# Latent attention heads in one pipeline over three token pieces, with values weighed by unsplit fp32 matmuls

## The chip, the cores and the metric

The kernel runs on one core of one Trainium2 chip. Its engines are TensorE (PE in the profile; PEld is its weight load), VectorE (DVE), ScalarE (ACT), GpSimd (POOL) and the DMA queues. The metric is the time of one execution on the device in microseconds. The kernel before takes 3545.39 us (median of 3 runs, 3545.22 to 3548.24).

## The reference, cut to what matters

A first block (windowed attention, convolution, a recurrence, a wide feed-forward) is followed by two layers that each contain latent attention. The change is in the heads of those two layers; the rest is the same code.

```python
T = 1040 tokens (16 meta tokens and 1024), 8 heads, 2 layers, all float32
q  = (c_q  @ w_q_b ).reshape(T, 8, 96)            # c_q : 768 channels, normalised
kv = (c_kv @ w_kv_b).reshape(T, 8, 64 + 64)       # c_kv: 256 channels, normalised
k_nope, v = kv[..., :64], kv[..., 64:]
k  = concatenate([k_nope, k_rope of all heads])   # 96 wide
q, k = rmsnorm(q), rmsnorm(k)                     # over the 96
q, k = rope on the last 32 of each
s = q @ k.T / sqrt(96), causal                    # 1040 x 1040 for each head
o = softmax(s) @ v
y_mla = (o * silu(z_mla)) @ mla_w_up
```

## The kernel before, in words

Activations lie with channels on partitions and tokens along the free dimension (1044 columns, the last four empty). An fp32 product is made of three matmuls with rounded operands (fp32r): high by high, high by low, low by high. The stored low part of an operand is the operand less its rounded value. Weights come as a stream of units of 128 x 1024. SyncE loads unit n+2 when GpSimd has split unit n; GpSimd casts a unit to its high part and subtracts for the low part (L322, L324), after TensorE has reported the unit two places before it as used. One unit holds a head's query and key/value weights.

Each engine has an order of instructions written out by hand, tied by semaphores; nothing is reordered by a planner. PSUM has `acc`, two slots of three banks, and `aux`, two banks. In the head stage (8 heads in each of 2 layers) a head is done so:

- `head_key_value`, `head_query` (L578, L583; matmuls at L353): 24 weight tiles, each over three pieces of 348 tokens, into one slot each. ScalarE squares and copies the whole width (`head_key_squares`, `head_query_squares`), TensorE sums squares with a matrix of ones in plain fp32 (`head_sum`, L587, L591), ScalarE takes log and exponential (`head_log`, L1066, and `head_exp`, L1072), VectorE applies the rope table, the scale and the split of query and key (`head_table`, `head_query`, `head_key`, L1601 to L1621, over 1044 columns at once).
- `rough_scores` (L605, matmuls L613, L617): high parts alone, rows of 128 queries, to get an upper row maximum; VectorE reduces (`maxima`, L1662). `head_values` transposes the values (L601), which ScalarE and VectorE store as V1 and V2. The nine columns of maxima are turned into one row (L686) that is put into an unused row of the query, so that later scores come with their maximum subtracted.
- `scores_t` (L620, matmuls L629, L633): scores transposed, keys on partitions, three matmuls per tile. There are 15 blocks of at most 384 columns (`BLOCKS`), in five batches of three; batch b has slot 1 - b % 2. ScalarE computes each block's exponential twice, once as fp32 and once rounded (L1145, L1146); VectorE subtracts for the low part (`low_parts`, L1648).
- `weigh_values` (L637, matmuls L648): three matmuls per tile into `aux`; the other 64 columns of V1 are ones, so the sum of a row comes with it. `head_inverse` (ScalarE) and `head_out` (VectorE, L1659, L1660) divide.

The next head's key, query and sums stand between rough scores and scores of this head; the last six blocks' values stand inside the next head's rough scores. VectorE waits once in each layer for the spill of `work` to memory (`g_spilled`) after its first `head_table`.

## Time and profile before

| | us |
|---|---|
| median of 3 runs | 3545.39 |
| lowest, highest | 3545.22, 3548.24 |
| span of the profiled execution | 3557.2 |
| PE busy | 3139.6 |
| DVE busy | 1569.9 |
| ACT busy | 711.5 |
| POOL busy | 833.7 |

For the profiled execution only its span is given, from its first to its last instruction, and that span is the profiled execution's own time here. It is 11.8 us above the median of the runs. Busy is the time in which an engine has a record; a TensorE record contains the delay until its result is written, so consecutive records overlap and the distance of their starts is the cost of one. The two head stages lie at about 1901 to 2320 us and 2987 to 3408 us. The mean granted clock of TensorE over the span is 0.929, where 1.00 is 2.4 GHz and 0.50 is 1.2 GHz.

### The profile page before, as it was taken

To read this page: it belongs to the slowest core of one execution; us is meant where nothing else is said; L and a number is where in the kernel's file an instruction comes from. 1 tells how busy PE (TensorE), PEld (TensorE's weight loads), DVE (VectorE), ACT (ScalarE), POOL (GpSimd) and SP (SyncE) were. 2 spreads that over 40 slices of the span, in tenths; PEclk is the share of its full clock that TensorE was granted. 3 is DMA by queue.
4 is the path that set the end of the run, shared out by engine and by line. 5 is a ranking of instruction groups with operands and counts; after the bars stand their busy time and mean duration, and the time that the engine had idled before them with its cause. 6 is when DMAs were issued, how large, how long until landed. Compare 5 with 4: busy or idle time off the path is not lost.

```text
span 3557.2 us, 40295 instructions
## 1 busy us (share of the span) xinstructions
PE 3139.6 (88%) x16640; PEld 2803.0 (79%) x16640; DVE 1569.9 (44%) x1540; ACT 711.5 (20%) x1191; POOL 833.7 (23%) x646
## 2 busy tenths in 40 slices
PE   6975676999999995999997888898999997888899
PEld 4754565777777774999997787798999997877789
DVE  4677456333333336500115665663520114655671
ACT  2132310000000002000112454400000111544410
POOL 2321012233333331333322000022333332000012
PEclk9987789999999997999998888899999998988899
DMA  2100011111111111112112000042112112000131
GB/s 98 47 30 27 0 71 38 47 46 43 47 47 41 47 47 66 54 42 96 48 42 77 8 13 13 31 152 94 42 48 90 48 42 84 13 13 7 37 145 71
DMA packets 46201, 182.47 MB, mean 51 GB/s; under 512 B 5744, under 2 KB 5872, under 8 KB 45552
## 3 DMA queue, kind: packets, MB, share of 16 engines
q1 hardware_dynamic: 31248, 113.19, 10.0%
q10 hardware_dynamic: 14816, 67.28, 4.9%
q8 instruction: 108, 1.77, 0.2%
q14 instruction: 29, 0.24, 0.0%
HBM read 150.06 MB, written 30.39 MB: 51 GB/s over the span
## 4 chain that ended last, share of the span: by engine, by line
PE 70%; DVE 20%; ACT 4%; issue 3%; DMA 1%; POOL 1%; DVEq 0%; ACTq 0%; SPq 0%; POOLq 0%
PE acc L353 61%; PE aux L648 2%; DVE act_lo L1214 2%; DVE ff_split L1214 2%; DVE small L1665 2%; DVE ff_split L1213 1%; DVE residual L1279 1%; PE acc L629 1%; PE acc L613 1%; DVE act_hi L1213 1%; DVE work L1230 1%; DMA spill_g<-work 1%; DVE work L1223 1%; ACT pool_split L1146 1%; PE aux L686 1%
## 5 line engine op out<-in xcount | busy, mean ns | idle before, releaser
L353 PE MATMUL acc<-act_hi,w_hi 128*128 128x348 f32 (+1 forms) x3488 | 868.4, 351 | 106.0 <-DVE act_lo L1214 39.2
L353 PE MATMUL acc<-act_lo,w_hi 128*128 128x348 f32 (+1 forms) x3488 | 855.7, 347 | 0.0
L353 PE MATMUL acc<-act_hi,w_lo 128*128 128x348 f32 (+1 forms) x3488 | 853.0, 346 | 0.0
L353 PEld LDWEIGHTS acc<-act_hi,w_hi 128*128 128x128 f32 x3488 | 619.3, 193 | 168.1 <-issue 70.5
L321 POOL TENSOR_TENSOR small<-shape_consts 128x1 f32<-128x1 f32 x212 | 47.1, 222 | 2666.4 <-PE acc L353 2666.4
L353 PEld LDWEIGHTS acc<-act_lo,w_hi 128*128 128x128 f32 x3488 | 624.4, 193 | 44.0
L353 PEld LDWEIGHTS acc<-act_hi,w_lo 128*128 128x128 f32 x3488 | 620.8, 192 | 42.1
L324 POOL TENSOR_TENSOR w_lo<-w_raw,w_hi 128x1024 fp32r<-128x1024 f32 x212 | 568.1, 2680 | 17.0
L353 PE MATMUL acc<-ff_split,w_hi 128*128 128x512 f32 (+1 forms) x1408 | 356.6, 379 | 22.0 <-DVE ff_split L1214 22.0
L1431 DVE TENSOR_TENSOR residual<-acc,residual 128x1024 f32<-128x1024 f32 (+1 forms) x88 | 108.1, 1229 | 468.2 <-PE acc L353 468.2
L353 PEld LDWEIGHTS acc<-ff_split,w_hi 128*128 128x128 f32 x1408 | 257.6, 190 | 71.1 <-DVE ff_split L1214 26.5
L322 POOL CAST w_hi<-w_raw 128x1024 fp32r<-128x1024 f32 x212 | 220.8, 1041 | 0.0
L648 PE MATMUL aux<-pool_split 128*128 128x276 f32 (+5 forms) x864 | 154.1, 332 | 60.7 <-DVE pool_split L1648 60.5
L353 PE MATMUL acc<-ff_split,w_lo 128*128 128x512 f32 (+1 forms) x704 | 202.4, 376 | 0.0
L648 PEld LDWEIGHTS aux<-pool_split 128*128 128x128 f32 x864 | 136.6, 217 | 68.8 <-DVE pool_split L1648 41.6
L629 PE MATMUL acc<-ff_split 128*128 128x276 f32 (+5 forms) x864 | 165.8, 336 | 1.9 <-issue 1.9
L957 ACT ACTIVATE work<-acc 128x1024 f32<-128x1024 f32 x32 | 32.8, 1028 | 642.5 <-PE acc L353 641.9
L629 PEld LDWEIGHTS acc<-ff_split 128*128 128x128 f32 x864 | 150.7, 221 | 5.5 <-issue 2.6
L1223 DVE TENSOR_TENSOR work<-work 128x1044 f32<-128x1044 f32 (+1 forms) x47 | 73.4, 1562 | 174.1 <-ACT work L763 172.9
L353 PEld LDWEIGHTS acc<-ff_split,w_lo 128*128 128x128 f32 x704 | 129.6, 189 | 23.9
L1665 DVE TENSOR_REDUCE small<-acc 128x1 f32<-128x128 f32 (+2 forms) x144 | 116.9, 812 | 67.7 <-PE acc L617 62.6
L613 PE MATMUL acc<-ff_split 128*128 128x512 f32 (+4 forms) x240 | 91.3, 460 | 57.9 <-DVE small L1665 30.6
(215 smaller groups left out, 2887.3 us busy)
## 6 DMA issues: line engine op xcount, KB each, us to landing
w_raw<-in_wstream SPq DMA_DIRECT2D x215, 512.0 KB, 3.5
spill_x<-residual ACTq DMA_DIRECT2D x2, 4176.0 KB, 12.7
spill_m<-residual ACTq DMA_DIRECT2D x2, 4176.0 KB, 13.2
spill_g<-work ACTq DMA_DIRECT2D x2, 4176.0 KB, 14.3
residual<-spill_m ACTq DMA_DIRECT2D x16, 522.0 KB, 5.9
work<-spill_g ACTq DMA_DIRECT2D x16, 522.0 KB, 7.9
residual<-spill_x ACTq DMA_DIRECT2D x16, 522.0 KB, 4.3
residual<-in_xT ACTq DMA_DIRECT2D x8, 512.0 KB, 9.9
```

Of the source, the lines that this page charges most:

```text
L321: nc.gpsimd.tensor_tensor(S_[:, 62:63], C_[:, 128:129], C_[:, 128:129], ALU.add)
L322: nc.gpsimd.tensor_copy(Wh[:, s, :], Wraw[:, s, :]).then_inc(sems["w_hi_done"], 1)
L324: nc.gpsimd.tensor_tensor(Wl[:, s, :], Wraw[:, s, :], Wh[:, s, :].bitcast(F32), ALU.subtract).then_inc(sems["w_lo_done"], 1)
L353: ins = nc.tensor.matmul(acc[0:m, s, p, 0:w], wt[:, ws, w0 + j * m:w0 + j * m + m], x[:, k, p * w:p * w + w], start=(first and t == 0), st ...
L613: ins = nc.tensor.matmul(acc[:, s, p, 0:n], qh[:, min(P * i, LASTQ):min(P * i, LASTQ) + P], kh[:, 512 * p:512 * p + n], start=True, stop=n ...
L629: ins = nc.tensor.matmul(out, k2[kt][:, c0:c0 + P], q2[qt][:, lo:lo + w], start=m == 0, stop=(m == 2 and not diag))
L648: ins = nc.tensor.matmul(aux[:, pc % 2, lo - QP * pc:lo - QP * pc + w], v[:, t, :], prob(n, part)[:, at:at + w], start=(t == 0 and m == 0) ...
L1213: do(vec.tensor_copy(hi, src))
L1214: do(vec.tensor_tensor(lo, src, hi.bitcast(F32), ALU.subtract), name)
L1223: do(vec.tensor_tensor(total, total, slots[1 + j % 2][:, cols], ALU.add), "sum_ready" if j == n - 1 else "sq_free" if j <= n - 3 else "dve ...
L1431: do(vec.tensor_tensor(x, acc_view(s, pieces), x, ALU.add), f"free{s}")
L1665: do(vec.tensor_reduce(S_[:, 16 + i:17 + i], acc[:, s, :, :].rearrange("p a b -> p (a b)")[:, 0:min(P * (i + 1), TP)], AX, ALU.max, negate ...
```

## The change

The head stage is written again for all engines. Tokens go in three pieces of 384, 384 and 276 columns (`QP`, `NQP`, which existed for the blocks). `acc` is used by bank: `acc_q`, `acc_k`, `acc_n` (sums and turned values), two of scores `acc_s`, and `acc_r` (rough scores, one bank, a rough row of over 512 keys in two or three parts with a maximum each). A pass over `h` runs through the 15 blocks of head h and, beside block n, does a fixed part of the preparation of head g = h + 1; a pass h = -1 comes first. The values of block n - 2 are weighed in step n. Every hand-over has its own semaphore, where `free`/`ready` pairs and `to_dve` were shared.

Probabilities are written once, as plain fp32 (`prob(k)`, a ring of 6), and the values once for each of two heads (`values(h)`); one matmul takes both as they are. The second exponential, `low_parts` and V2 are gone. Temporary arrays of a piece's width have two buffers. GpSimd's loop over weight units is cut into loops and single splits around the heads, without other waits. The wait for `g_spilled` stands before VectorE's first table operation.

Core of the diff (TensorE):

```diff
-                        for m, (v, part) in enumerate(((V1, 0), (V1, 1), (V2, 0))):
-                            ins = nc.tensor.matmul(aux[:, pc % 2, lo - QP * pc:lo - QP * pc + w], v[:, t, :],
-                                                   prob(n, part)[:, at:at + w],
-                                                   start=(t == 0 and m == 0), stop=(end and m == 2))
+                        ins = nc.tensor.matmul(aux[:, b % 2, lo - QP * pc:lo - QP * pc + w], values(h)[:, t, :],
+                                               prob(k)[:, at:at + w], start=t == 0, stop=end)
...
+                for h in range(-1, MH):
+                    g = h + 1
+                    more = g < MH
+                    for n in range(NB):
+                        if h >= 0:
+                            scores(h, n)
+                            if n == 0:
+                                turn_maxima(h, 1)
+                            if n in (1, 2, 3):
+                                rough_scores(h, 5 + n, 0)
+                            if n == 4:
+                                rough_scores(h, 8, 2)
+                            if n == 5:
+                                turn_maxima(h, 2)
+                        if more:
+                            if n in (8, 9, 10):
+                                rough_scores(g, n - 8, 0)
+                            if n == 11:
+                                turn_maxima(g, 0)
+                            if n in (12, 13, 14):
+                                rough_scores(g, n - 9, 0)
+                            if n in (0, 4, 8):
+                                key_value_part(g, n // 4)
+                            elif n < 12:
+                                query_part(g, n // 4, n % 4 - 1)
+                            if n in (3, 7, 11):
+                                key_sum(g, n // 4)
+                            if n in (4, 8, 12):
+                                query_sum(g, n // 4 - 1)
+                            if n in (6, 10, 13):
+                                turn_values(g, (n - 6) // 3)
+                            if n in (13, 14):
+                                rough_scores(g, n - 9, 1)
+                        if h >= 0 and n in (1, 2, 3):
+                            rough_scores(h, 5 + n, 1)
+                        if h >= 0 and n >= 2:
+                            weigh_values(h, n - 2)
+                        if h >= 1 and n < 2:
+                            weigh_values(h - 1, NB - 2 + n)
```

Waits of a sum, of the turned maxima and of the turned values (one bank each, `n_free` and `r_free` being the last reader):

```diff
+                def query_sum(g, pc):
...
+                    pe.wait_ge(*n_free[0])
+                    pe.wait_ge(sems["q_squared"], k)
+                    nc.tensor.matmul(acc_n[:, 0:w], ones96, qsq[k % 2][:, 0:w], start=True,
+                                     stop=True).then_inc(sems["q_sum"], 1)
+                    n_free[0] = (sems["qn_free"], k)
...
+                def turn_maxima(h, pc):
...
+                    pe.wait_ge(*r_free[0])
+                    if pc:
+                        pe.wait_ge(sems["max_ready"], 2 * (l * MH + h) + pc)
...
+                def scores(h, n):
...
+                    if k > 2:
+                        pe.wait_ge(sems["p_in"], k - 2)
+                    if tiles[0][0] == 0:
+                        pe.wait_ge(sems["max_row"], wave(l, h, pc))
+                        pe.wait_ge(sems["k_lo"], wave(l, h, pc))
+                        pe.wait_ge(sems["q_lo"], wave(l, h, pc))
```

ScalarE's order and VectorE's order in the same steps:

```diff
+                            exponents(h, n)
+                            if n == 0:
+                                maximum_row(h, 1)
+                            if n == 2 and h >= 1:
+                                inverse_sums(h - 1, 2)
+                            if n == 4:
+                                inverse_sums(h, 0)
+                            if n == 5:
+                                maximum_row(h, 2)
+                            if n == 9:
+                                inverse_sums(h, 1)
...
+                            if n == 11:
+                                maximum_row(g, 0)
+                            if n in (4, 8, 12):
+                                key_scale(g, n // 4 - 1)
+                            if n in (0, 4, 8):
+                                key_value_evict(g, n // 4)
+                            if n in (5, 9, 13):
+                                query_scale(g, n // 4 - 1)
+                            if n in (7, 11, 14):
+                                values_in(g, (n - 7) // 3)
+                            if n in (3, 7, 11):
+                                query_squares(g, n // 4)
...
+                            if n == 3 and h >= 1:
+                                head_out(h - 1, 2)
+                            if n in (1, 2, 3):
+                                maximum(h, 5 + n, 0)
+                                maximum(h, 5 + n, 1)
+                            if n == 4:
+                                maximum(h, 8, 2)
+                                maxima_of(2)
+                            if n == 5:
+                                head_out(h, 0)
+                            if n == 10:
+                                head_out(h, 1)
...
+                            if n in (4, 8, 12):
+                                query_table(g, n // 4 - 1)
+                            if n in (5, 9, 13):
+                                key_norm(g, n // 4 - 1)
+                            if n in (6, 10, 14):
+                                query_norm(g, (n - 6) // 4)
+                            if n in (8, 9, 10):
+                                maximum(g, n - 8, 0)
+                            if n in (12, 13, 14):
+                                maximum(g, n - 9, 0)
+                            if n in (13, 14):
+                                maximum(g, n - 9, 1)
+                            if n == 14:
+                                maxima_of(1)
```

`query_table` is three VectorE operations on a piece (rope table from PSUM, a copy of 32 rows, an addition on 32 rows), `key_norm` four, `query_norm` three, `head_out` two.

## Rows read from the trace of the kernel before

**Rows 1.** The page: busy us (share of the span) and instructions of each engine.
```profile
PE 3139.6 (88%) x16640; PEld 2803.0 (79%) x16640; DVE 1569.9 (44%) x1540; ACT 711.5 (20%) x1191; POOL 833.7 (23%) x646
```

**Rows 2.** Stretches of one head; PEclk is the granted clock.
```profile
core 0: us, PE busy (x) PEld busy (x) DVE busy (x) ACT busy (x) POOL busy (x), PEclk, DMA share, GB/s
1971.05:2022.24 51.19, 45.05 (x254) 40.78 (x253) 30.75 (x42) 24.16 (x50) 3.53 (x3) 0.87 0.04 11
2008.59:2012.01 3.42, 1.95 (x12) 1.75 (x10) 3.32 (x4) 2.79 (x7) 0.00 (x0) 1.00 0.00 0
2018.83:2022.24 3.41, 1.39 (x11) 1.39 (x12) 3.24 (x6) 1.33 (x5) 0.00 (x0) 1.00 0.00 0
2022.24:2025.66 3.42, 3.42 (x18) 3.42 (x17) 0.89 (x2) 1.54 (x4) 0.00 (x0) 0.50 0.00 0
2032.48:2035.90 3.42, 1.90 (x9) 1.16 (x7) 3.28 (x5) 0.00 (x0) 0.00 (x0) 1.00 0.00 0
2035.90:2039.31 3.41, 3.14 (x10) 2.95 (x11) 2.68 (x3) 0.00 (x0) 0.00 (x0) 0.50 0.02 5
```

**Rows 3.** Waits of that head: us in total, times, longest.
```profile
POOL small L321 <- PE acc L353: 47.7, 1, 47.7
PE aux L648 <- DVE pool_split L1648: 3.9, 2, 2.3
PEld acc L613 <- DVE small L1665: 3.2, 5, 1.4
PE acc L613 <- DVE small L1665: 2.2, 4, 1.2
```

**Rows 4.** Timeline of TensorE at full clock: start, us, record.
```profile
2051.37 0.64 PE L353 MATMUL acc<-act_lo,w_hi 128*128 128x348 f32 x3
2051.85 0.63 PE L353 MATMUL acc<-act_hi,w_lo 128*128 128x348 f32 x3
2052.32 1.92 PE L591 MATMUL acc<-residual,shape_consts 128*128 128x348 f32 x6
2054.16 1.91 PE L686 MATMUL aux<-shape_consts,small 128*1 128x128 f32 x18
2056.00 2.02 PE L591 MATMUL acc<-residual,shape_consts 128*128 128x348 f32 x6
...
2277.79 0.45 PE L629 MATMUL acc<-ff_split 128*128 128x20 f32 x3
2278.10 0.26 PE L633 MATMUL acc<-pool_split 128*128 128x20 f32 x1
...
2280.41 1.54 PE L648 MATMUL aux<-pool_split 128*128 128x276 f32 x12
...
2298.32 2.32 PE L629 MATMUL acc<-ff_split 128*128 128x384 f32 x12
```

**Rows 5.** Groups of that head by form: busy us, mean ns, idle before.
```profile
L1648 DVE TENSOR_TENSOR pool_split<-work,pool_split 128x384 fp32r<-128x384 f32 x7 | 3.9, 558 | 0.4 <-ACT pool_split L1146 0.2
L1145 ACT ACTIVATE work<-acc 128x384 f32<-128x384 f32 x7 | 3.5, 497 | 1.0 <-DVE pool_split L1648 0.8 <-PE acc L629 0.3
L1648 DVE TENSOR_TENSOR pool_split<-work,pool_split 128x276 fp32r<-128x276 f32 x7 | 3.1, 446 | 0.4
L1213 DVE CAST ff_split<-residual 128x1044 fp32r<-128x1044 f32 x2 | 1.4, 704 | 0.1
L1610 DVE SCALAR_TENSOR_TENSOR residual<-residual,params 128x1044 f32<-128x1044 f32 x1 | 1.3, 1305 | 0.0
L1665 DVE TENSOR_REDUCE small<-acc 128x1 f32<-128x512 f32 x1 | 0.7, 692 | 0.0
L1092 ACT ACTIVATE work<-work 64x384 f32<-64x384 f32 x1 | 0.5, 523 | 0.0
```

**Rows 6.** Timeline around GpSimd's split of a unit, and the copy alone.
```profile
1892.02 3.33 DVE L1214 TENSOR_TENSOR act_lo<-work,act_hi 128x1044 fp32r<-128x1044 f32 x1
...
1909.24 0.69 DVE L1603 COPY residual<-residual 32x1044 f32<-32x1044 f32 x1
...
2052.69 1.04 POOL L322 CAST w_hi<-w_raw 128x1024 fp32r<-128x1024 f32 x1
2053.81 2.35 POOL L324 TENSOR_TENSOR w_lo<-w_raw,w_hi 128x1024 fp32r<-128x1024 f32 x1
2054.94 1.77 DVE L1603 COPY residual<-residual 32x1044 f32<-32x1044 f32 x1
```

**Rows 7.** Timeline at the start and end of the head stage of layer 0.
```profile
1916.00 0.43 DVE L1679 CAST pool_split<-shape_consts 128x512 fp32r<-128x512 f32 x1 [4.80 <-DMA spill_g<-work]
...
2319.73 0.57 PE L353 MATMUL acc<-ff_split,w_hi 128*128 128x348 f32 x2
```

More of the change, by code:

```diff
@@ L620, in scores_t, with key_value_part @@
-                def scores_t(n, s, b, q2, k2):
+                n_free, r_free = [None], [None]
+                def key_value_part(g, pc):
+                    k = wave(l, g, pc)
+                    c0, w = QP * pc, piece_width(pc)
+                    if pc == 0:
+                        w_head[0] = ws()
+                        next_unit()
+                    if k > 1:
+                        pe.wait_ge(sems["k_free"], k - 1)
+                    for j in range(2):
+                        if g == 0 and pc == 0:
+                            pe.wait_ge(sems["a_ready"], a_count + j + 1)
+                        for t, (wt, x) in enumerate(((Wh, Ah), (Wh, Al), (Wl, Ah))):
+                            ins = nc.tensor.matmul(acc_k[:, 0:w], wt[:, w_head[0], (6 + j) * P:(7 + j) * P],
+                                                   x[:, 6 + j, c0:c0 + w], start=(j == 0 and t == 0),
+                                                   stop=(j == 1 and t == 2))
+                    ins.then_inc(sems["kv_raw"], 1)
@@ new lines, in query_part @@
+                def query_part(g, pc, part):
+                    k = wave(l, g, pc)
+                    c0, w = QP * pc, piece_width(pc)
+                    if part == 0 and k > 1:
+                        pe.wait_ge(sems["q_free"], k - 1)
+                    for j in (2 * part, 2 * part + 1):
+                        if g == 0 and pc == 0:
+                            pe.wait_ge(sems["a_ready"], a_count + j + 3)
+                        for t, (wt, x) in enumerate(((Wh, Ah), (Wh, Al), (Wl, Ah))):
+                            ins = nc.tensor.matmul(acc_q[:, 0:w], wt[:, w_head[0], j * P:j * P + P],
+                                                   x[:, j, c0:c0 + w], start=(j == 0 and t == 0),
+                                                   stop=(j == 5 and t == 2))
+                    if part == 2:
+                        ins.then_inc(sems["q_raw"] if pc < NQP - 1 else sems["unit_done"], 1)
@@ new lines, in key_sum @@
+                def key_sum(g, pc):
+                    k = wave(l, g, pc)
+                    c0, w = QP * pc, piece_width(pc)
+                    if n_free[0] is not None:
+                        pe.wait_ge(*n_free[0])
+                    pe.wait_ge(sems["k_squared"], k)
+                    nc.tensor.matmul(acc_n[:, 0:w], ones96, X[:, 6, c0:c0 + w], start=True,
+                                     stop=True).then_inc(sems["k_sum"], 1)
+                    n_free[0] = (sems["kn_free"], k)
@@ new lines, in turn_maxima @@
+                def turn_maxima(h, pc):
+                    pe.wait_ge(*r_free[0])
+                    if pc:
+                        pe.wait_ge(sems["max_ready"], 2 * (l * MH + h) + pc)
+                    for i in range(3 * pc, 3 * pc + 3):
+                        n = min(P, TP - P * i)
+                        o = P * (i - 3 * pc)
+                        ins = nc.tensor.matmul(acc_r[32:33, o:o + n], S_[:, 16 + i:17 + i], ident[:, P - n:P],
+                                               start=True, stop=True)
+                    ins.then_inc(sems["max_turned"], 1)
+                    r_free[0] = (sems["max_row"], wave(l, h, pc))
@@ L622, in scores_t @@
                     at = 0
-                    for j, lo, w in BLOCKS[n][1]:
-                        out = acc[:, s, b, at:at + w]
+                    for j, lo, w in tiles:
+                        out = acc_s[k % 2][:, at:at + w]
                         at += w
@@ L1651, in head_out @@
                 def head_out(h, pc):
[L1653 to L1655 removed]
+                    k = wave(l, h, pc)
+                    dve.wait_ge(sems["inv_ready"], k)
                     w = piece_width(pc)
@@ L1723, in _ @@
-                low_parts(4)
-                head_out(MH - 1, 1)
+                for h in range(-1, MH):
+                    g = h + 1
+                    more = g < MH
+                    for n in range(NB):
+                        if h >= 0:
+                            if n == 3 and h >= 1:
[10 more added lines that the diff above has]
+                                head_out(h, 1)
+                            if n in (6, 8) and not more:
+                                j = n // 2 - 3
+                                split(X[:, j, :], Fy[0][:, j, wide], Fy[1][:, j, wide], "f_ready")
+                        if more:
+                            if n in (4, 8, 12):
[12 more added lines that the diff above has]
+                                maxima_of(1)
```

579 lines of the change are left out of this document (259 added, 320 removed).

## The prediction

> **What bounds the kernel now.** I read the page's busy times first, then the TensorE clock by stretches of one head, then the waits of that head, then its timeline. TensorE is busy for 3139.6 us of a span of 3557.2 [rows 1], so time can come only from its work, its clock or its gaps. The change touches one stage, the attention heads: 16 heads (8 in each of two layers), about 51.2 us each. In one such head (the first of [rows 2]) TensorE has 45.05 us of records and 6.1 us without any, and a mean granted clock of 0.87. The short stretches say where: in three of those shown TensorE has records for 1.95, 1.39 and 1.90 of 3.4 us. After the first the clock stays at 1.00 (2.4 GHz); the other two are followed by 0.50 (1.2 GHz), each time for two stretches of 3.4 us. 13.6 us per head at 1.2 GHz, nearly all filled, cost half of that, 6.7 us. So a head is 38.3 us of work at full clock, 6.7 us of low clock and 6.2 us of gaps. The gaps are hand-overs [rows 3]: the first weighing of values in a piece waits for VectorE's low parts (3.9 us), rough scores for VectorE's maxima (2.2 us on TensorE, 3.2 on its weight loads).
>
> **The change part by part.** All durations are starts to starts at full clock.
>
> 1. *Values product.* Removed: 36 of 54 matmuls per head, 15 ScalarE exponentials (the second copy), 15 VectorE subtractions (about 7.3 us busy; 0.56 and 0.45 us each [rows 5]) and the value low parts. Added: nothing but the matmul's own kind. The rounded form costs 0.16 us per 348 columns (three start 0.48 apart), 0.175 at 384 (twelve in 2.32 us), 0.13 at 276, and does not fall below 0.103 for 20 columns (three, then the next start 0.31 us later) [rows 4]. The unrounded form appears as two records per matmul; six records of 348 columns take 1.92 us to the end of the last, 1.84 to the next start, so 0.29 a record and 0.58 a matmul, 0.64 at 384, 0.46 at 276; at 128 columns 18 records take 1.84, so 0.21 a matmul [rows 4]. A head has 18 tiles: 5 of 384, 7 of 276, 2 of 256, 4 of 148 or less. Before: 3 x (5 x 0.175 + 7 x 0.13 + 2 x 0.122 + 4 x 0.105) = 7.4 us. After: 5 x 0.64 + 7 x 0.46 + 2 x 0.427 + 0.9 = 8.1 us. So the product itself gets 0.7 us per head slower; bounds 0 (if the small tiles hide their weight loads) and +2.5 (below).
> The Trainium skill ("FP8 and Floating Point Precision", section "TensorE Precision Notes") says that true fp32 takes four passes through the array. Four in place of three would make it 7.4 x 4/3 = 9.9 us, +2.5. The rows above say +0.7, because the rounded form pays a floor on small tiles that the unrounded one does not; I take the rows, and +2.5 is a rival below.
>
> 2. *Pieces.* Query, key and sum matmuls become 384, 384 and 276 columns wide where they were 348 three times: 24 groups of 0.175 + 0.175 + 0.13 = 0.48 us, as before. Nothing. Rough scores, transposes and causal adds are the same instructions. TensorE's work by the new order, summed over its 15 steps: scores 8.3, values 8.1, rough 3.5, turned maxima 1.9, query and key 11.5, sums 3.5, turned values 0.8: 37.8 us.
>
> 3. *One pipeline.* Each step issues scores of block n, a part of the next head and the values of block n-2. So the gaps must be found again. A hand-over TensorE to X to TensorE costs X plus some 0.3 us (the tail of the last record and two starts). I walked one head with ScalarE at 0.49 us (384) and 0.40 (276), VectorE at 0.56 and 0.45 (0.62 for the scaled product and 0.36 for a cast at 384, brought down from 1.31 and 0.70 at 1044 by the slope of the rows; 0.69 for a maximum over 512) [rows 5], and VectorE's and ScalarE's queues in the order of the diff. What ends late:
> - n=4: the query sum waits until ScalarE has read the key sum, and ScalarE has the exponential (0.49) and the inverse of the sums (0.49 and 0.52) ahead of that 0.49: 1.0 us.
> - n=8: the same without the inverse: 0.15.
> - n=11: the maxima are turned only when VectorE has reduced rough tile 2, behind the head output and the query of piece 1: 1.0; then the key sum behind ScalarE's copies: 0.3.
> - n=12, 13: query sum behind ScalarE (0.7), turned values behind ScalarE (0.8), rough tile 4's second half (0.2).
> - n=14: the second half of rough tile 5 behind VectorE's query of piece 2 and a maximum: 1.1.
> Together 5.3 us of gaps, and VectorE, 27.8 us busy by the same rows, is the late one from n=10 to n=14, where it has 10.9 us of work beside 10.0 us of TensorE's (PE steps n=10 to 14).
>
> 4. *GpSimd.* It splits one weight unit per head: cast 1.04 us, subtraction 2.35 us, started by the end of the head's query product [rows 6]. While it runs, VectorE operations that read only SBUF stand: a copy of 32 x 1044 takes 1.77 us beside it and 0.69 alone, and a subtraction of 1044 takes 3.33 where 1.25 is usual [rows 6]. The new order ends the query product at n=11, right ahead of VectorE's rope addition for piece 2 and all that follows, which is the late chain: +2.1 us (bounds 0 and 2.4). The loop over units cut in several costs nothing: GpSimd waits 47.7 of 51.2 us [rows 3].
>
> A head is then 37.8 + 5.3 + 2.1 = 45.2 us at full clock.
>
> 5. *First and last pass.* VectorE starts at 1916.0 when the spill has landed, as before [rows 7], now ahead of its first query. The first pass has no scores to fill it; VectorE's 20 us come in a chain with TensorE's and ScalarE's at low clock: I get the first scores at 1947.8. Seven passes of 45.2 less 0.9 (the first has no old head to finish), and a last pass of 24.2 us (8.3 + 8.1 + 1.8 + 1.2 us of work, and three steps with two maxima each, 1.0 us of waiting apiece, 1 us at the end): 1947.8 + 315.5 + 24.2 = 2287.5. Before, the next stage's matmuls start at 2319.7 [rows 7]. That is 32 us for a layer, 64 for both (I take layer 1 to repeat it).
>
> 6. *Clock.* From n=11 to n=14 of the new order TensorE has 7.8 us of work in 14.1. Its thinnest stretches resemble those of 1.95 and 1.90 us above, of which one kept the clock and the other lost it. One fall of 6.8 us there costs about 2.2 us, since part of it lies in gaps. Bounds: 0 and 2 falls in filled work, 6.7 us. I take a fall in half of the heads: 1.1 x 14 = 15 us.
>
> Sum: 64 - 15 = 49 us off the profiled 3557.2. That execution is 11.8 us above the median of the three runs, 0.3%; taken off the median 3545.4 it gives 3496.
>
> **The rivals.**
> - *Clean pipeline.* GpSimd's hold misses VectorE's chain and the clock stays: 43.1 us a head. For it: VectorE's total is far below TensorE's. Against: the split starts exactly there. 64 + 2 x 15 = 94 off: 3452.
> - *Slower: the clock is lost in filled work.* Many short waits keep TensorE thin enough, from n=9 until the next head's query parts, to be at 1.2 GHz for as long as now (13.6 us a head, 6.7 us lost), all of it beside dense work, on top of 45.2: 51.9. The first pass already costs 21.6 us that the old order did not have before its first scores (against 10 won in the last). 7 x 51.9 = 363.3 against 315.5 + 0.9: 47 more than above in a layer, 15 slower than before (32 won): 3545 + 30 = 3575. It decides from 49.8 us a head, where the 32 us of a layer are used up. For it: two of three thin stretches lose the clock now. Against: the dense steps n=0 to n=8 have no gap over 1 us.
> - *Four passes.* The unrounded product costs 9.9 us in a head: 1.8 x 16 = 29 more: 3525. Against: the 0.29 us record of 348 columns; for: full-width weights are loaded for each record, which the 128-column row has not.
> - *It does not do what it says*: the gaps and low clock only move, since TensorE's work is no less than now (37.8 us against 38.3), and a head ends near 49.8. That is 3545, no change. Against: the walk finds 7.4 us of gaps where 12.9 are now lost.
>
> **How the numbers follow.** Forecast 0.55 (3496, own range 3470 to 3525), clean 0.18 (3452), four passes 0.12 (3525), lost clock 0.12 (3575), no change 0.03. Below 3435 would need a head under 42 us, 4 of gaps. Range 3435 to 3560, which leaves out most of the lost clock and a little of the clean case. A change under 0.2% (7 us) can't be told from none. Faster: 0.84 (a little of the third case lost to its spread); same 0.04; slower 0.12.
>
> **What would show it.** The values matmuls: 36 records a head, 0.23 us apart at 276 columns and 0.32 at 384, not more. The distance of the same instruction in neighbouring heads: 45 to 46.5 us; under 44 clean, over 49.8 slower. A VectorE addition over 32 rows of about 2.5 us once a head beside GpSimd's subtraction. TensorE's waits in n=11 to n=14 on VectorE, in n=4 on ScalarE. Clock 1.00 through n=0 to n=8. The first scores 21 us later than the first rough scores now, the stage's end 2285 to 2300 in layer 0. Wrong would be: waits at each score for exponentials (I have none), or values products waiting for GpSimd.

## The result and the profile after

| | median us | lowest, highest | runs |
|---|---|---|---|
| kernel before | 3545.44 | 3539.79, 3548.24 | 6 |
| changed kernel | 3557.70 | 3554.25, 3560.82 | 6 |

The ratio is 1.0039 (95% interval 1.0027 to 1.0052): slower by 12 us, where 3496 was forecast; 3557.7 lies just inside the stated range of 3435 to 3560. The profiled execution of the changed kernel has a span of 3556.4 us and a time of 3558.25, typical of its runs. In all runs the time is 1.8 to 1.9 us above the span, so the profiled execution of before [rows 1], with a span of 3557.2, took about 3559 and lay 14 us above its median, and not 11.8. The two profiles therefore show about the same length though the medians do not.

First the stretches, with the columns of [rows 2]: two heads of the changed kernel from one GpSimd cast to the next, then four short stretches of the head at 2018 to 2069 us in order of time, nearly end to end.

```profile
1978.03:2027.42 49.39, 43.88 (x235) 35.61 (x236) 28.06 (x54) 23.29 (x53) 3.40 (x2) 0.93 0.04 11
2078.20:2129.18 50.98, 45.49 (x235) 37.04 (x236) 28.04 (x54) 23.29 (x53) 3.40 (x3) 0.90 0.04 11
...
2030.40:2033.80 3.40, 1.76 (x11) 1.14 (x9) 3.19 (x7) 1.22 (x3) 0.50 (x1) 1.00 0.49 142
2033.84:2037.24 3.40, 2.78 (x11) 2.53 (x11) 2.12 (x5) 0.00 (x0) 0.00 (x0) 0.53 0.02 10
2037.24:2040.64 3.40, 2.55 (x9) 1.82 (x8) 1.28 (x3) 0.68 (x3) 0.00 (x0) 0.50 0.00 0
2040.64:2044.04 3.40, 3.40 (x13) 2.37 (x12) 0.00 (x0) 0.97 (x2) 0.00 (x0) 0.50 0.03 7
```

A head takes 49.9 us on average in layer 0 (seven casts apart, 48.4 to 51.0), against 51.2 in the head of [rows 2]. TensorE is at 1.2 GHz once in every head, for 6.8 us (the heads of about 49.4) or 10.2 us (those of about 51.0), and the last of the short stretches is full of records: the low clock lies on dense work. In the head of [rows 2] it was 13.6 us.

TensorE's waits on VectorE and ScalarE in the head at 2078 us, as in [rows 3]: us in total, times, longest.

```profile
PE acc L709 <- DVE small L1783: 3.2, 3, 1.7
PE acc L683 <- ACT head_out L1204: 1.0, 1, 1.0
PE acc L726 <- DVE small L1783: 0.8, 1, 0.8
PE acc L683 <- ACT residual L1204: 0.6, 1, 0.6
```

The 3.9 us for low parts in [rows 3] are gone; rough tiles (L709) still wait for maxima, and the sums (L683) and turned maxima (L726) have waits of their own. The timeline of TensorE through n = 11 to 14 (L726 turned maxima, L683 query sum, L709 rough scores; the wait before each stands in brackets):

```profile
2025.51 0.82 PE L726 MATMUL acc<-shape_consts,small 128*1 128x128 f32 x6 [0.79 <-DVE small L1783]
...
2029.70 0.73 PE L683 MATMUL acc<-residual,shape_consts 128*128 128x276 f32 x2 [0.57 <-ACT head_out L1204]
...
2031.97 0.49 PE L709 MATMUL acc<-ff_split 128*128 128x512 f32 x1 [0.64 <-DVE small L1783]
...
2034.46 0.47 PE L709 MATMUL acc<-ff_split 128*128 128x128 f32 x1 [1.67 <-DVE small L1783]
...
2039.16 0.58 PE L709 MATMUL acc<-ff_split 128*128 128x256 f32 x1 [0.85 <-DVE small L1783]
```

And VectorE and GpSimd in the same stretch, beside [rows 6]:

```profile
2027.42 1.04 POOL L342 CAST w_hi<-w_raw 128x1024 fp32r<-128x1024 f32 x1 [45.91 <-PE acc L660]
2028.54 2.35 POOL L344 TENSOR_TENSOR w_lo<-w_raw,w_hi 128x1024 fp32r<-128x1024 f32 x1
```

```profile
2028.29 0.32 DVE L1750 COPY work<-residual 32x276 f32<-32x276 f32 x1
2028.65 2.54 DVE L1751 TENSOR_TENSOR residual<-residual,work 32x276 f32<-32x276 f32 x1
2031.23 0.69 DVE L1783 TENSOR_REDUCE small<-acc 128x1 f32<-128x512 f32 x1
```

The addition at L1751 takes 2.54 us beside GpSimd's subtraction (0.43 without it, in the version with the later split below), and the maximum for which TensorE waits at 2031.97 comes behind it.

The stage's ends, to set against [rows 7]: the landing of the spill, the first scores, the first scores of the last head, and the next stage's matmuls.

```profile
1912.25 0.43 DVE L1806 COPY work<-shape_consts 128x512 f32<-128x512 f32 x1 [12.53 <-DMA spill_g<-work]
...
1940.40 1.27 PE L751 MATMUL acc<-ff_split 128*128 128x384 f32 x3
...
2291.39 1.55 PE L751 MATMUL acc<-ff_split 128*128 128x384 f32 x3
...
2317.05 1.20 PE L405 MATMUL acc<-ff_split,w_hi 128*128 128x348 f32 x6
```

The stage of layer 0 ends 2.7 us earlier than before (2319.7), and the spill landed 3.8 us earlier: from the landing it is 404.8 us against 403.7. In layer 1 the same two differences leave 2.2 us (3405.8 against 3408.0) and again about one more from the landing.

### The profile page after: what moved, and what is told of

Its sections match the earlier page's. It is cut to its first block, busy times and chain, and to the rows that moved or that the text cites. A ratio compares the mean times of both kernels' runs of the same rounds, so it can differ in the third digit from the quotient of the medians.

```text
span 3556.4 us, 40398 instructions
## 1 busy us (share of the span) xinstructions
PE 3141.6 (88%) x16352; PEld 2739.0 (77%) x16352; DVE 1527.6 (43%) x1730; ACT 699.6 (20%) x1239; POOL 828.6 (23%) x626
## 4 chain that ended last, share of the span: by engine, by line
PE 74%; DVE 17%; issue 3%; ACT 3%; DMA 1%; POOL 1%; DVEq 0%; ACTq 0%; SPq 0%; POOLq 0%
PE acc L405 56%; PE aux L772 3%; PE acc L660 3%; PE acc L751 3%; DVE act_lo L1356 2%; DVE small L1783 1%; PE acc L709 1%; DVE residual L1421 1%; PE acc L726 1%; DVE residual L1751 1%; PE acc L645 1%; DVE act_hi L1355 1%; DVE work L1372 1%; DVE work L1365 1%; PE acc L683 1%
## 5 line engine op out<-in xcount | busy, mean ns | idle before, releaser
L405 PE MATMUL acc<-act_hi,w_hi 128*128 128x348 f32 (+1 forms) x3104 | 772.0, 349 | 103.8 <-DVE act_lo L1356 39.6
L405 PE MATMUL acc<-act_lo,w_hi 128*128 128x348 f32 (+1 forms) x3104 | 762.8, 346 | 0.0
L405 PE MATMUL acc<-act_hi,w_lo 128*128 128x348 f32 (+1 forms) x3104 | 761.6, 346 | 0.0
L405 PEld LDWEIGHTS acc<-act_hi,w_hi 128*128 128x128 f32 x3104 | 546.9, 191 | 163.7 <-issue 66.4
L405 PEld LDWEIGHTS acc<-act_lo,w_hi 128*128 128x128 f32 x3104 | 549.5, 190 | 43.9
L405 PEld LDWEIGHTS acc<-act_hi,w_lo 128*128 128x128 f32 x3104 | 546.1, 190 | 41.9
L1783 DVE TENSOR_REDUCE small<-acc 128x1 f32<-128x512 f32 (+4 forms) x240 | 132.1, 551 | 197.6 <-PE acc L709 137.7
L772 PE MATMUL aux<-work 128*128 128x276 f32 (+5 forms) x576 | 187.9, 424 | 0.0
L1247 ACT ACTIVATE work<-acc 128x384 f32<-128x384 f32 (+2 forms) x240 | 104.5, 436 | 339.2 <-PE acc L751 168.9
L709 PE MATMUL acc<-ff_split 128*128 128x512 f32 (+4 forms) x240 | 103.8, 432 | 65.9 <-DVE small L1783 65.7
L874 ACT ACTIVATE work<-acc 64x384 f32<-64x384 f32 (+5 forms) x153 | 93.7, 621 | 326.8 <-PE acc L405 266.6
```

Of the source, the lines that this page charges most:

```text
L405: ins = nc.tensor.matmul(acc[0:m, s, p, 0:w], wt[:, ws, w0 + j * m:w0 + j * m + m], x[:, k, p * w:p * w + w], start=(first and t == 0), st ...
L709: ins = nc.tensor.matmul(acc_r[:, 0:n], qh[:, min(P * i, LASTQ):min(P * i, LASTQ) + P], kh[:, 512 * p:512 * p + n], start=True, stop=not diag)
L772: ins = nc.tensor.matmul(aux[:, b % 2, lo - QP * pc:lo - QP * pc + w], values(h)[:, t, :], prob(k)[:, at:at + w], start=t == 0, stop=end)
L874: return nc.scalar.activation(out, in_, ACT.Copy, scale=scale)
L1247: do(nc.scalar.activation(prob(k)[:, 0:w], src, ACT.Exp), "p_in")
L1783: do(vec.tensor_reduce(S_[:, col:col + 1], acc_r[:, 0:n], AX, ALU.max, negate=True), "rough_max")
```

## The experiments

The theory after the result: the new order has too many short hand-overs between n = 11 and 14; GpSimd's hold lengthens them, and the clock that they cost lies on dense work. The unsplit product is good by itself. The rival: the chain scores, exponentials, values now sets the head, or the plain fp32 product is dearer than the rows said, and gaps and clock only follow. The versions ran on three chips; each ratio is to runs of the kernel before on the same chip (medians 3546 to 3549). The head's length is the distance of GpSimd's casts in one trace; where the heads differ, their range stands in the table.

| kernel | us | ratio to before, 95% | a head, us | clock in it |
|---|---|---|---|---|
| changed, GpSimd later | 3509.2 | 0.989 (0.986 to 0.992) | 47.8 | 0.93 |
| changed, extra multiplications | 3514.3 | 0.990 (0.987 to 0.993) | 46.8 | 1.00 |
| changed, values first | 3541.8 | 1.000 (0.998 to 1.002) | 48.4 to 50.0 | 0.90 to 0.93 |
| changed, later and first | 3485.7 | 0.983 (0.979 to 0.987) | 44.7 to 46.2 | 0.93 to 0.98 |
| changed, all three | 3471.3 | 0.977 (0.974 to 0.980) | 44.3 | 1.00 |
| changed, one rounded product | 3504.6 | 0.987 (0.984 to 0.990) | 45.8 to 47.2 | 0.89 to 0.93 |
| before, unsplit product | 3452.9 | 0.973 (0.968 to 0.979) | 44.3 | 0.92 |
| the same, extra multiplications | 3422.7 | 0.964 (0.961 to 0.967) | 42.3 | 1.00 |
| the same, values spread | 3419.5 | 0.963 (0.960 to 0.966) | 41.2 | 1.00 |
| the same, spread further | 3411.7 | 0.961 (0.960 to 0.963) | 40.7 | 1.00 |
| before, values spread | 3506.5 | 0.988 (0.986 to 0.990) | 45.3 to 47.8 | 0.93 to 1.00 |

### GpSimd's split later

```diff
+                    pool.wait_ge(sems["max_turned"], wave(l, h, 1))
```

ahead of each head's split, so that it falls behind the rope additions.

> The changed kernel, with one more wait on GpSimd: in the head stages it splits the next weight unit only after the maxima of the next head's second piece are turned (step n=0 of the next pass), where VectorE has mostly maxima that read PSUM. Theory (a head of 50.8 us is 37.8 of TensorE work, 5.3 of hand-over gaps, 2.1 behind GpSimd's hold on VectorE, about 4 of low clock in filled work): the 2.5 us addition over 32 rows goes back to 0.43, the head loses 2.1 us at least, and up to 6 if the thin stretch gets short enough to keep the clock; 14 heads: 3475 to 3528 against 3557.7. Rival (the hold is hidden behind ScalarE or TensorE): under 10 us of change, over 3548.

48 us less than the changed kernel at the median; its runs spread from 3493.3 to 3520.8, and the profiled one, with a span of 3516.8, is 40 us under the changed kernel's. In that one the head fell from 49.9 to 47.8. VectorE's addition is back at its own length (its timeline, with the copy before it):

```profile
2023.19 0.29 DVE L1751 COPY work<-residual 32x276 f32<-32x276 f32 x1
2023.51 0.43 DVE L1752 TENSOR_TENSOR residual<-residual,work 32x276 f32<-32x276 f32 x1
```

The addition is 2.1 us shorter, which is what the prediction gave the hold, in VectorE's late chain, where it was put. The head's 2.1 us are not the hold alone: the clock still falls once a head (0.93), now always for the shorter time. Against the changed kernel's heads with the same clock (49.4 us) the gain is 1.6 us.

### Extra multiplications ahead of the waits

```diff
+                                fill(h, n, 5)
...
+                    for _ in range(count):
+                        nc.tensor.matmul(acc_s[(k + 1) % 2][:, 0:276], key[:, 0:P], q[:, 768:1044],
+                                         start=True, stop=True)
```

In all 5 multiplications at n = 11, 3 at 12, 4 and 12 at 13, 5 at 14, ahead of the waits there.

> The changed kernel with 29 more matmuls of 276 columns a head (3.8 us of work at full clock), in front of five of TensorE's waits of n=11 to n=14; their results are overwritten by the next scores. Theory (TensorE is thin there and so drops to 1.2 GHz for 6.8 to 10.2 us, which reaches into the filled steps n=0 and n=1): the clock stays at 1.00 in most heads, and the head gets shorter by 2 to 4 us although it does more work; 3500 to 3530. Rival (the steps n=13 to n=0 are long because of VectorE's chain, the clock only follows): no gain, or up to 3.8 us more a head, 3555 to 3610.

One head:

```profile
2072.66:2119.43 46.77, 45.14 (x264) 37.64 (x265) 28.05 (x54) 23.28 (x53) 3.41 (x3) 1.00 0.04 13
```

TensorE does 29 useless matmuls a head, some 3.8 us at 0.13 each (the price of [rows 4] at 276 columns), and the head is 3.1 us shorter. Nothing else of the work, of its order or of VectorE's (28.05 us busy as before) has changed; only the clock has, from 0.90 or 0.93 to 1.00. Most of the waits are filled by the added work (in this head 0.98 us at n = 4 and 0.26 us at n = 14 are left). The low clock is thus a cost of its own and not a picture of the gaps.

### Values first in their step

```diff
+                            if n >= 2:
+                                weigh_values(h, n - 2)
+                            elif h >= 1:
+                                weigh_values(h - 1, NB - 2 + n)
...
-                        if h >= 0 and n >= 2:
-                            weigh_values(h, n - 2)
```

right behind the scores, ahead of the next head's parts.

> The changed kernel with TensorE's values product of block n-2 moved to right behind the scores of block n, so ahead of the step's waits. Theory (gaps are hand-overs of 0.6 to 1.7 us of fixed length): each of the six gaps gets up to 0.46 to 0.64 us shorter, 2 to 3 us a head, and the clock may stay: 3500 to 3535. Rival (VectorE's chain of n=11 to n=14 sets the pace, whatever TensorE does between): the gaps only move, under 1 us a head, 3545 to 3558.

16 us from the changed kernel, between the two expectations, and at the kernel before's own time (ratio 1.000). In the head at 2074 us one wait of 1.06 us before the first half of rough tile 4 stands in place of 0.57 before the query sum and 0.64 there, 0.79 becomes 0.63, 0.97 becomes 0.33, and those of 1.67 and 0.85 stay. Work placed ahead of a wait shortened some waits and left others as they were.

### The two together, and all three

> The pipeline kernel with GpSimd's split after the third turned maximum and the values of a block first in its step, no extra multiplications. The two alone took 48 us (3509) and 16 us (3542); with 23 extra multiplications on top they gave 3471. Theory (a low-clock stretch stays as long as TensorE has an idle stretch in the hand-over, and costs 2 to 3.5 us a head): 3490 to 3515, the head 47 to 48 with the granted clock at 0.92 to 0.94. Rival (with both edits the gaps are short enough and the clock does not fall; the extra multiplications did nothing there): 3465 to 3480, the head 44 to 45.

> The pipeline kernel with the three edits together: GpSimd's head split after the third turned maximum, the values of a block issued first in its step, and 23 extra multiplications a head ahead of the waits at n = 11 to 14, which leave the clock no idle stretch. Theory (hold, gaps and low clock are separate costs that overlap only in part): the GpSimd edit alone gave a head of 47.8, the extra multiplications alone 46.8 at full clock; together they should give about 43 to 45 a head, 3440 to 3480 us in all, with the granted clock at 0.99 or 1.00. Rival (the chain from scores through exponentials to values sets the head, whatever fills it): not under 46.5 a head, 3505 or more.

The head with the two edits, then with all three (23 extra multiplications, 3.0 us of them):

```profile
2078.34:2124.03 45.69, 42.80 (x235) 34.29 (x235) 25.90 (x54) 23.28 (x53) 3.42 (x2) 0.94 0.04 12
```

```profile
2077.71:2122.00 44.29, 43.44 (x258) 36.41 (x259) 25.91 (x54) 23.30 (x53) 3.42 (x2) 1.00 0.04 13
```

The gains add up, and a little more: 48 and 16 us alone, 72 together. The two edits came in below the theory's interval (3490) and above the rival's (3480), and so did the heads (44.7 to 46.2 us, where 47 to 48 and 44 to 45 were expected): the clock still falls, for less. With all three TensorE has 0.85 us of a head without a record and the chain scores, exponentials, values does not show, so that rival is out. Yet 3471 is still 18 us above the old order with the same product (next section), and none of that lies in the full heads, which take 44.3 us in both. It lies at the ends of a layer: with all three edits the time from the landing of the spill to the first scores is 27.5 us and from the last head's first scores to the next stage 24.7, 52.2 together, against 44.3 for one more head of the old order.

### The old order with the unsplit product

```diff
-                        for m, (v, part) in enumerate(((V1, 0), (V1, 1), (V2, 0))):
...
+                        ins = nc.tensor.matmul(aux[:, pc % 2, lo - QP * pc:lo - QP * pc + w], V1[:, t, :],
+                                               prob(n, 0)[:, at:at + w], start=t == 0, stop=end)
```

with `low_parts`, V2 and the second exponential removed, and nothing else of the change; the semaphores that VectorE raised behind its low parts are raised by ScalarE.

> The kernel before with one part of the change alone: probabilities and values stored once as plain fp32 and multiplied by one matmul; the second exponential, VectorE's low parts and the values' low parts are gone, the order of everything else is as before. Theory (the product costs 0.7 us more on TensorE, and 3.9 us of its gaps wait for low parts): a head gets 3 us shorter and perhaps one of its two low-clock stretches goes, 1.5 to 3.4 more: 3445 to 3500 against 3545.4. Rival (four passes make the product 2.5 us dearer and something else ends as late): 3540 to 3590.

One head, two stretches around its low clock, and TensorE at the wait that comes ahead of it:

```profile
2035.15:2079.52 44.37, 42.24 (x236) 36.43 (x235) 22.32 (x25) 19.39 (x35) 3.52 (x5) 0.92 0.05 13
2058.40:2061.80 3.40, 2.08 (x9) 1.45 (x9) 3.15 (x6) 0.00 (x0) 0.00 (x0) 1.00 0.00 0
2061.80:2065.20 3.40, 2.87 (x8) 2.33 (x9) 2.96 (x4) 0.00 (x0) 0.00 (x0) 0.51 0.00 0
```

```profile
2062.10 1.22 PE L613 MATMUL acc<-ff_split 128*128 128x512 f32 x2 [1.20 <-DVE small L1648]
```

This is the main finding. The product alone takes 93 us off, and the pipeline in which it was wrapped gives back 105: 5.6 us in each of 14 heads (49.9 against 44.3), the rest at the ends of the two layers. Per head: 3.9 us of waits for low parts go [rows 3], one of the two low-clock stretches of 6.8 us goes with them (3.4 us), and the product costs the 0.7 us of the prediction: 51.2 - 3.9 - 3.4 + 0.7 = 44.6, measured 44.3.

### The old order, its clock kept

The same kernel with 13 matmuls of 384 columns ahead of rough-score groups 4 to 7:

```diff
+                        if h and 4 <= i < 8:
+                            aux_free[1].wait(pe)
+                            for _ in range((3, 2, 6, 2)[i - 4]):
+                                nc.tensor.matmul(aux[:, 1, 0:384], k2[0][:, 0:P], q2[0][:, 0:384],
+                                                 start=True, stop=True)
```

> The order of the kernel before with the unsplit values product, and 13 extra multiplications of 384 columns a head (about 2.1 us at full clock) ahead of the rough-score groups 4 to 7, where TensorE waits 1.8 us a head and then runs 6.8 us at the low clock. Theory (the one low stretch of a head is set off by the rough-score gaps and costs about 3 us): the clock stays at 1.00, the head falls from 44.3 to 41 to 42.5, the whole to 3400 to 3430. Rival (the clock falls whatever is done, or the extra work costs as much as the clock gives back): 3445 to 3465.

and with real work there in their place:

```diff
-                        if h and i < 2:
-                            for n in BATCHES[3 + i]:
+                        if h:
+                            for n in {0: BATCHES[3], 1: BATCHES[4][:1], 3: BATCHES[4][1:2],
+                                      5: BATCHES[4][2:]}.get(i, ()):
                                 weigh_values(n)
...
-                        if h and i == 4:
+                        if h and i == 8:
                             head_out(h - 1, 2)
```

> The order of the kernel before with the unsplit values product, and the last two value blocks of the head before moved from behind the second rough-score group to behind the fourth and the sixth, where TensorE otherwise waits for VectorE's maxima; VectorE's last head_out moves behind the ninth maximum. No work is added. Theory: the 1.2-us wait in rough scores goes, and with it some or all of the low clock; 41 to 43.5 a head, 3400 to 3440. Rival (the wait only moves to the maxima): 3445 to 3460.

Moving two value blocks by a few steps takes 33 us off and keeps the clock at 1.00; no instruction is added or removed. Spread further, with both `head_out` of the head before behind the last maximum:

```diff
+                            for n in {0: (9, 10), 1: (11,), 2: (12,), 3: (13,), 5: (14,)}.get(i, ()):
+                                weigh_values(n)
```

> The order of the kernel before with the unsplit product and the value blocks spread thinner (two, one, one, one, none, one behind the rough-score groups 0, 1, 2, 3 and 5), both head_outs of the head before behind the ninth maximum. Against the first spread version (3420) it takes 1.1 us a head off VectorE's chain of maxima, for which TensorE still waits 1.7 us a head. Theory: half a microsecond to one a head off, 3405 to 3414. Rival (the wait moves to the transposes of the values, which need the accumulator that head_out frees): 3416 to 3425.

```profile
2071.30:2111.95 40.65, 39.36 (x236) 33.66 (x235) 22.41 (x25) 19.12 (x35) 3.52 (x4) 1.00 0.05 14
```

3411.7 us, 134 under the kernel before and 146 under the changed one, is the fastest version found. TensorE has 1.3 us of a head without a record.

### The old order and old product, values spread

> The kernel before, low parts and all, with the last two value blocks of a head moved from behind the second rough-score group to behind the fourth and the sixth, and the last head_out behind the ninth maximum. With the unsplit product this order took 33 us off (3453 to 3420). Theory: the rough-score gap and the low-part waits are separate; this takes 1.5 to 3 us off a head but leaves the waits of 1.7 and 2.3 us for the low parts and a low-clock stretch behind them: 3500 to 3525. Rival (the low parts set the pace, the moved blocks wait for their own low parts): 3535 to 3550.

3506.5: the same edit is worth 42 us here. In layer 0 most heads take 47.4 to 47.8 with the clock at 0.93: of two low-clock stretches one is gone, and the other stays, right behind the second wait for low parts (1.65 and 2.29 us in its timeline). So each of the two groups of waits can have its own low-clock stretch. But the waits alone do not decide it. In layer 1 every second head keeps the clock at 1.00 with the same two waits for low parts. One head of each kind, and the two waits of the second:

```profile
2046.05:2093.73 47.68, 42.11 (x254) 38.08 (x253) 30.67 (x42) 24.26 (x50) 3.52 (x4) 0.93 0.04 12
3062.69:3107.95 45.26, 39.21 (x254) 34.84 (x253) 30.75 (x42) 23.88 (x50) 3.53 (x5) 1.00 0.04 12
```

```profile
3073.32 1.98 PE L648 MATMUL aux<-pool_split 128*128 128x384 f32 x12 [1.64 <-DVE pool_split L1649]
...
3081.99 1.72 PE L648 MATMUL aux<-pool_split 128*128 128x256 f32 x12 [2.32 <-DVE pool_split L1649]
```

What makes the difference between these heads, 2.4 us, no run here shows.

### One rounded product in the new order

Probabilities and values stored rounded and multiplied once; their low parts are left out of the computation.

```diff
-            return R_[:, o:o + QP]
+            return G_[:, o - 8 * RW:o - 8 * RW + QP]
```

(G_ holds rounded numbers, R_ plain ones; the same for the values.)

> The pipeline kernel with probabilities and values stored rounded and multiplied once in that form: the low parts and so their accuracy are left out. TensorE has 4.8 to 5.4 us less work a head than in the pipeline kernel. If TensorE's work set the head (the prediction's view), the head falls from 49.9 to about 45 and the whole by 80 us, to 3475. If gaps, hold and low clock set it, less work only makes longer gaps: the granted clock falls below 0.90, the head loses 1 to 3 us, and the whole comes to 3510 to 3545.

```profile
2067.66:2113.47 45.81, 39.08 (x217) 32.03 (x218) 28.05 (x54) 23.30 (x53) 3.41 (x2) 0.93 0.04 12
```

53 us less, with a head of 46.3 us on average in layer 0 where it took 49.9, for about 5 us less work of TensorE a head; I had expected 3510 to 3545 if gaps and clock set the pace and 3475 if work did, and it lies between. About two thirds of the removed work show, and the rest turns into gaps (6.7 us of this head are without a record, 5.5 in the changed kernel's head of 49.39). The unsplit product is not to blame: with about two thirds of its time gone by the prices of [rows 4], the new order does not reach the old one's 3453.

### The kernel before, profiled once more

> The kernel before, unchanged, one profile more: its profiled run was 12 us above its median. If the head of a typical run has the same waits with a shorter low-clock stretch, it shows 50.2 to 50.8 us instead of 51.2, at the same busy counts.

It took 3544.9. No head between two casts shows the expected 50.2 to 50.8 us. In layer 0 they are as in [rows 2] but for the last, 49.3, and that one was 49.2 in the first profile too; in layer 1 they differ. One of each:

```profile
2052.88:2104.14 51.26, 45.10 (x254) 40.84 (x253) 30.65 (x42) 24.22 (x50) 3.51 (x4) 0.87 0.04 11
3228.51:3278.55 50.04, 43.74 (x254) 39.15 (x253) 30.65 (x42) 24.22 (x50) 3.51 (x4) 0.90 0.03 11
```

In the profile of [rows 1] the six heads between two casts in layer 1 took 50.3 once and 51.1 to 51.3 otherwise; here they take 47.4 to 50.0. Together they are 294.1 us instead of 306.3. The last head, from its cast to the next stage, takes 64.9 instead of 68.4, and the two spans differ by 14.1 us, so the surplus of the first profile lies in the heads of layer 1.

## Why the prediction was wrong

**The failed step is number 6, the clock.** It took one fall in half of the heads at 2.2 us, 1.1 us a head. The trace shows a fall in every head, of 6.8 or 10.2 us, and more of it on dense work than the prediction had. In the head at 2018 to 2069 us step n = 14 takes 4.70 us, and n = 0 takes 4.85 (from the first score matmul of one step to that of the next), where the prediction's prices give about 2.8 for each (in n = 14 with the wait of 1.1). That is 3.9 us in two steps that lie at 1.2 GHz almost to their end. The prediction's upper bound of 6.7 holds it; its rule for the middle did not ("thinnest stretches resemble those of 1.95 and 1.90 us, of which one kept the clock"). It read a doubt as one half, where the trace shows a fall in every head, in this one during the fourth of the waits of n = 11 to 14, the one of 1.67 us. And it put part of the fall into gaps; but the clock stays low after the waits are over, until 2044.0, into the next head's key product. Its sentence "the dense steps n=0 to n=8 have no gap over 1 us" was true and beside the point. The extra multiplications show that the clock is a cause and not a companion: the head got 3.1 us shorter, although they are 3.8 us of work themselves, most of it in place of waits.

The Trainium skill ("TensorE: Matmul & The Clock Gate", section "Part 1: The HAM clock gate (the "warmup" mystery)") says that the slow clock is the default and activity what lifts it. The runs agree in this: multiplications that compute nothing keep the granted clock at 1.00 (head of 46.77 us above).

**Steps 1 to 4 held, but for 1.7 us a head.** The query sums at 2018.5 and 2069.3 in the changed kernel are 50.8 us apart, and that is 45.2 + 3.9 + 1.7. The last term is in the other thirteen steps. 0.5 of it is the end of n = 13, which is at 1.2 GHz already (1.12 us from 2034.46 on, about 0.6 at full clock); where the rest lies, no run separates. It is not small: the average head, 49.9 us, leaves 3.0 for the clock beside the 1.7, so over 14 heads, as an estimate, the clock cost 42 us where 15 were forecast, and the 1.7 us another 24 where nothing was.

The waits were nearly those of the walk: n = 11 0.79 us (1.0 forecast), n = 12 0.57 (0.7), n = 14 0.85 (1.1), and 0.97 at n = 4 (1.0). At n = 13 the size was right and the place was not: the walk had 0.8 on the turned values behind ScalarE and 0.2 on rough tile 4, and the trace has none before the turned values and two for VectorE's maxima, 0.64 and 1.67, of which the hold was to bring 2.1. Two sums of the prediction don't come out of their terms: TensorE's work adds up to 37.6 and not 37.8 us, and six records of 348 columns in 1.84 us are 0.31 each and not 0.29; with 0.31 the product would have been priced at about +1.2 us and not +0.7. The trace of the changed kernel bears out the smaller price. The hold was there, the addition at 2.54 us, on the instruction that was named.

The unsplit product costs what the prediction had. At 384 columns one tile and the three rounded score matmuls of 276 behind it take 1.02 us to the next start, of which the latter are 0.39:

```profile
2067.16 0.81 PE L772 MATMUL aux<-work 128*128 128x384 f32 x2
2067.51 0.84 PE L751 MATMUL acc<-ff_split 128*128 128x276 f32 x3
2068.18 0.22 PE L709 MATMUL acc<-ff_split 128*128 128x128 f32 x1
```

That leaves the 0.64 of the prediction. The rival "four passes" was priced wrongly and is no rival: 0.64 us at 384 columns and 0.46 at 276 are four times 384 and 276 columns at 2.4 GHz (0.160 and 0.115 us). The passes that the Trainium skill states ("FP8 and Floating Point Precision", section "TensorE Precision Notes") are these; I had counted them as 4/3 of three rounded matmuls, which each carry some 15 ns more than their columns.

**Step 5 nearly held in its ends and not in its sum.** First scores came at 1940.4 (1947.8 forecast), the last pass took 25.7 us (24.2), the seven between 351.0 (315.5): minus 7.4, plus 1.5, plus 35.5, so the stage ends 29.6 us later than the 2287.5 of that step, and all but a few of the 32 us of a layer are gone. (The terms given for the last pass add up to 23.4, not 24.2.) The point of turning was put at 49.8 us a head, and the head came out at 49.9: the sum was right about where it decides.

**The baseline.** The saving was worked out from heads of 51.2 us. That execution was 14 us above the median, and the second profile of before puts the surplus in the heads of layer 1. The prediction took its saving off the median without the surplus, which assumes that the changed kernel would have the same surplus in such an execution. It had none: its profile is at its median. That is some 13 us of the miss of 62; the other 48 are the saving of 49 between the two spans, of which 0.8 came.

**The rivals.** "The clock is lost in filled work" was the right mechanism, with 6.8 to 10.2 us of low clock a head where it said 13.6 and 3.0 us lost on average where it said 6.7, at a chance of 0.12; "it does not do what it says", with a head near 49.8 and 3545, was the nearest in time, at 0.03.

**What the prediction never asked** is what each half of the change does alone. Its own rows held the answer: 3.9 us a head of waits for low parts, with a low-clock stretch behind them, and a product that costs 0.7 more. That is 6.6 us a head or 105 in all, of which 93 were measured, without a new order. The new order then had to earn its place against 44.3 us and not against 51.2.

## What to carry to other kernels

Price each half of a combined change by itself, and set the second against what the first leaves. Where an engine's order has several short waits in a row, count the low clock behind them in full, on the dense work that follows (in the changed kernel it came in every head; in the kernel before with its values spread some heads kept their clock with the same waits), and look for work to move between the waits before building a new order: here two value blocks moved by a few steps were worth 33 us. Check first whether the profiled execution is at the median of its kernel, and take its heads, not only its total, as one sample.

## What was not expected of the hardware

- Useless matmuls made a kernel faster, in both orders: 29 of 276 columns a head took 43 us off (3557.7 to 3514.3), 13 of 384 columns took 30 off (3452.9 to 3422.7), each by keeping the granted clock at 1.00.
- The kernel before falls into several lengths (3531.8 to 3563.0 in 21 runs on one chip), while the versions whose clock stays at 1.00 in the heads after the first repeat within 3.3 us (3512.1 to 3515.4; 3422.0 to 3423.0; 3411.6 to 3414.1), and so does the old order with the unsplit product, which has one low stretch in each (3451.4 to 3453.7). The profiles of two lengths differ in how long the clock is low in the heads of layer 1.
- What was not tried: extra multiplications in the fastest version (its clock is at 1.00 in the six heads between two casts of a layer, 0.93 in the last stretch of a layer), and the new order with rough tiles in two banks, which might shorten the wait of 1.67 us rather than fill it.
